# A lane's shift in four parts with in-projection blocks between them, and a unit's first state ahead of its own-chunk sums

## The chip, the cores and the metric

The kernel runs on one NeuronCore of one Trainium2 chip. The metric is the device time of one execution in microseconds (us). Engines are named as in the profile: PE is TensorE, PEld its weight load, DVE is VectorE, ACT is ScalarE, POOL is GpSimd, SP is SyncE.

## The reference

Two transformer blocks on 256 tokens of width 2048. The change touches one stage, the even mixer of the first block (an RWKV-7 scan in both directions), for context and latent tokens:

```python
def rwkv_dir_inputs(r0, k0, v0, wd, ad, mu_rkv, mu_lora, w0, w2, a0, a2, k_k, k_a, reverse):
    sh = lambda u, mu: token_shift(u.astype(jnp.float32), mu, reverse)   # u + (nb - u) * mu
    r = sh(r0, mu_rkv[0]); k = sh(k0, mu_rkv[1]); v = sh(v0, mu_rkv[2])
    w_log = -jax.nn.softplus(-(w0 + jnp.tanh(sh(wd, mu_lora[0])) @ w2)) - 0.5
    decay = jnp.exp(-jnp.exp(w_log))
    a = jax.nn.sigmoid(a0 + sh(ad, mu_lora[1]) @ a2)
    kk = hd(k * k_k)
    kk = kk * lax.rsqrt(jnp.sum(jnp.square(kk), -1, keepdims=True) + 1e-12)
    k = k * (1.0 + (a - 1.0) * k_a)
    return (hd(r), hd(decay), hd(k), hd(v), -kk, kk * hd(a))
# wkv7_scan, step by step over the tokens:
#   sa = S a;  S = S * w + sa b^T + v k^T;  y = S r
```

The inputs `r0, k0, v0, wd, ad` and a gate come from the in-projection `h @ w_in`. The rest (pooling mixer, out-projection, attention block, then a whole second block) is not touched.

## The kernel before

`order_of_work` writes one list of steps by hand. Each engine's program then walks this list and emits the instructions that it has for each step, so the list sets the order of every engine's queue. Waits between engines are semaphores, found by name.

The stage of the change is a loop over **units**. A unit is one direction `d` (a *lane*, 0 forward, 1 backward), one pair of heads `hp` and one half `seg` (context or latent), with number n = 2 hp + seg: 16 units in each lane. The generator `unit` yields 22 times: `shift`, `kk_sum`, `keys`, `turn_AV`, `P_LR`, `KR0`, `KR1`, `double0` to `double5`, `solve`, `own`, `state0` to `state3`, `centre`, `gn_sum`, `read_out`. The two lanes go in rounds, lane 1 one step behind lane 0. At the end of each round `fill` emits a number of pieces of other work, by the table

```python
FILL = {"shift": 5.5, "kk_sum": 7.5, "keys": 6, "turn_AV": 3, ..., "own": 2, "state0": 2, ...}
```

That other work is the in-projection. A **block** here is one k-tile of one sum: three PE matmuls of 128x512 (`ev_times`: high by high, high by low, low by high). Its weights come through a ring by DMA, eight blocks to a **split** (`ev_split`): ACT copies 128x1024 to the high part, DVE subtracts to get the low part. A sum of 16 blocks ends in a **copy-out**, which frees the bank: ACT's `rkv_in` or `spill_out`, or for a gate ACT's `gate_in` (tanh of the bank) and then DVE's `gate_in` (a multiply that reads the bank). All these sums share one PSUM bank (bank 0), so the first block of a sum waits until the copy-out of the sum before is done. The other filling is `mod` (`mod_row` on ACT, `mod_col` on PE and DVE).

The steps that the change touches:

* `shift(d, n, b)`. ACT: three scaled copies (k, r, v), tanh of the decay row from PSUM bank `b`, square of k (`kk_sq`, which PE's `kk_sum` waits for), scaling of the decay row (`lw`), tanh and scaling of `ag`. DVE: three multiply-adds (k, r, v), a scan (L276 helper), `be`, `er`, three tiny operations for `dc`. ACT's `kk_sum` then takes exponentials of `be`, `er`, `dc`.
* `own_chunks(d, n)`: PE makes the products of each chunk in PSUM; DVE adds to them and writes `G` and `Q`; ACT copies `HY`.
* `state(d, n, i)`, i = 0 to 3: PE multiplies the running state `S` by `G` and `Q`; DVE adds `HY` and writes the next `S`. At i = 0 DVE first sets the unit's first state: a zero (`v.zero`, helper L273) for an even n, the old state times a decay (`v.ts`, helper L264) for an odd n. PE's `state` waits for it:

```python
pe.wait_ge(*at("S", d, n, i))
pe.wait_ge(*at("G", d, n))
pe.wait_ge(*at("Q", d, n))
```

* `read_out(d, n)`: PE turns the norm's factors, DVE does three operations of 128x256.

## Time and profile before

| what | value |
|---|---|
| median of 3 runs | 3706.95 us (3701.98 to 3708.23) |
| the profiled execution, its own time | 3699.59 us |
| its span in the profile | 3697.8 us |
| mean granted clock | 0.975 of full |
| stage of the 32 units | about 147 to 1300 us |

Read the page from the top: busy shares, then the stretch of the unit stage alone, then who waits for whom there, then the timeline around single waits. Since PE's queue is in order, an idle time of PE in a timeline is a delay of everything behind it.

### The profile page before, as it was taken

How to read it: one execution, taken by the hardware profiler on the slowest of the kernel's cores; microseconds unless marked ns; L12 is line 12 of the kernel's file. 1: busy time of each engine (PE TensorE's matmuls, PEld its weight loads, DVE VectorE, ACT ScalarE, POOL GpSimd, SP SyncE). 2: the span in 40 equal slices, each digit the busy share in tenths (PEclk: the TensorE clock that was granted, in tenths of full speed). 3: DMA queues.
4: the chain of work that ended last, by engine and by line, in shares of the span. 5: the costliest groups of instructions: out<-in, count | busy, mean ns of one | idle time of the engine just before them, and what ended most of it. 6: DMA issues, size and time to landing. Idle time of an engine off the chain costs nothing. (4 is left out here: it accounts for less than half of the span.)

```text
span 3697.8 us, 71036 instructions
## 1 busy us (share of the span) xinstructions
PE 3453.2 (93%) x31368; PEld 2866.8 (78%) x31368; DVE 2045.4 (55%) x3596; ACT 1549.5 (42%) x2596; POOL 249.0 (7%) x297
## 2 busy tenths in 40 slices
PE   7998899999899989899997999899999999999998
PEld 3676677777667757777886898569898899999787
DVE  2555555565556586755656566665444555555444
ACT  2433443443334433555544443444433444444333
POOL 0011101111111130020100001010000000000000
PEclk9999999999999999999998999999999999999999
DMA  9543423443344064433334543334544455555554
GB/s 378 192 120 105 130 86 110 119 123 99 97 121 122 23 239 157 149 113 103 109 137 152 191 149 126 114 117 159 191 160 141 167 182 178 178 181 183 182 193 159
DMA packets 349472, 548.57 MB, mean 148 GB/s; under 512 B 11724, under 2 KB 119916, under 8 KB 346988
## 3 DMA queue, kind: packets, MB, share of 16 engines
q1 hardware_dynamic: 346716, 538.78, 44.1%
q8 instruction: 246, 4.03, 0.4%
q10 hardware_dynamic: 2448, 5.24, 0.4%
q14 instruction: 62, 0.51, 0.0%
HBM read 535.86 MB, written 8.13 MB: 147 GB/s over the span
## 5 line engine op out<-in xcount | busy, mean ns | idle before, releaser
L301 PE MATMUL lane<-r,r 128*128 128x256 f32 (+1 forms) x8520 | 1504.2, 326 | 36.9 <-DVE r L259 27.3
L301 PEld LDWEIGHTS lane<-r,r 128*128 128x128 f32 x8520 | 1276.4, 192 | 195.8 <-DVE r L259 35.2
L301 PE MATMUL bank<-r,r 128*128 128x512 f32 (+2 forms) x6312 | 1374.0, 357 | 53.7 <-DVE arena L267 20.0
L259 DVE TENSOR_TENSOR r<-ring,r 128x1024 fp32r<-128x1024 f32 x770 | 939.9, 1227 | 824.3 <-ACT r L298 822.9
L301 PEld LDWEIGHTS bank<-r,r 128*128 128x128 f32 (+1 forms) x6312 | 1036.4, 193 | 252.6 <-ACT arena L298 32.9
L298 ACT ACTIVATE r<-ring 128x1024 fp32r<-128x1024 f32 x770 | 808.6, 1055 | 761.9 <-PE lane L301 587.2
L301 PE MATMUL lane<-arena 64*64 64x64 f32 (+5 forms) x13068 | 577.8, 251 | 59.3 <-issue 19.4
L301 PEld LDWEIGHTS lane<-arena 64*64 64x64 f32 (+2 forms) x13068 | 431.6, 138 | 211.8 <-issue 119.9
L298 ACT ACTIVATE arena<-lane 128x256 f32<-128x256 f32 (+3 forms) x543 | 242.7, 469 | 513.8 <-PE lane L301 278.0
L259 DVE TENSOR_TENSOR arena<-arena 128x256 f32<-128x256 f32 (+6 forms) x600 | 274.3, 486 | 34.1 <-ACT arena L298 12.5
L298 ACT ACTIVATE arena<-arena 128x256 f32<-128x256 f32 (+4 forms) x366 | 153.7, 451 | 224.8 <-DVE arena L259 111.8
L270 DVE COPY arena<-lane 128x256 f32<-128x256 f32 (+2 forms) x254 | 106.6, 421 | 170.6 <-PE lane L301 141.4
L259 DVE TENSOR_TENSOR arena<-lane,arena 128x256 f32<-128x256 f32 (+2 forms) x244 | 74.9, 333 | 190.7 <-PE lane L301 189.3
L259 POOL TENSOR_TENSOR arena<-arena,cm 128x4 f32<-128x4 f32 (+1 forms) x80 | 90.9, 1136 | 1042.3 <-ACT arena L298 668.7
L304 PE MATMUL lane<-cm,arena 128*128 128x128 f32 x744 | 117.4, 284 | 27.1 <-DVE arena L259 14.3
L259 POOL TENSOR_TENSOR arena<-arena 128x256 f32<-128x256 f32 (+3 forms) x134 | 122.2, 931 | 193.7 <-DVE arena L270 99.5
L301 PE MATMUL lane<-arena,cm 64*64 64x64 f32 (+2 forms) x1440 | 125.1, 232 | 4.9 <-DVE arena L264 4.3
L304 PEld LDWEIGHTS lane<-cm,arena 128*128 128x128 f32 x744 | 88.6, 145 | 49.6 <-DVE arena L259 16.2
L259 POOL TENSOR_TENSOR st<-st,cm 128x1 f32<-128x1 f32 (+2 forms) x19 | 12.7, 671 | 1694.5 <-DVE st L264 1694.5
L298 ACT ACTIVATE r<-arena 128x256 fp32r<-128x256 f32 (+2 forms) x143 | 67.7, 478 | 102.4 <-DVE arena L267 91.5
L267 DVE SCALAR_TENSOR_TENSOR arena<-arena,vec 128x256 f32<-128x256 f32 (+1 forms) x196 | 91.7, 494 | 28.0 <-ACT arena L298 24.6
L301 PEld LDWEIGHTS lane<-arena,cm 64*64 64x64 f32 (+1 forms) x1440 | 99.3, 142 | 8.5 <-issue 6.1
(94 smaller groups left out, 1260.8 us busy)
## 6 DMA issues: line engine op xcount, KB each, us to landing
ring<-in_w_gate_up SPq DMA_DIRECT2D x88, 1024.0 KB, 4.9
ring<-in_mod_w SPq DMA_DIRECT2D x73, 1024.0 KB, 5.2
ring<-in_ev_w_in SPq DMA_DIRECT2D x44, 1024.0 KB, 8.2
ring<-in_w_down SPq DMA_DIRECT2D x44, 1024.0 KB, 5.0
ring<-in_od_w_in SPq DMA_DIRECT2D x40, 1024.0 KB, 4.9
ring<-in_w_in SPq DMA_DIRECT2D x40, 1024.0 KB, 5.0
ring<-in_w_xkv SPq DMA_DIRECT2D x32, 1024.0 KB, 5.3
ring<-in_ev_w_out SPq DMA_DIRECT2D x28, 1024.0 KB, 5.2
```

Source lines behind the costliest of these rows:

```text
L259: return Nothing() if self.e is None else self.e.tensor_tensor(o, a, b, op)
L267: return Nothing() if self.e is None else self.e.scalar_tensor_tensor(o, a, s, b, op0, op1)
L270: return Nothing() if self.e is None else self.e.tensor_copy(o, a)
L298: return self.e.activation(o, a, f, bias=bias, scale=scale)
L301: return Nothing() if self.e is None else self.e.matmul(o, l, r, start=start, stop=stop)
L304: return Nothing() if self.e is None else self.e.transpose(o, a, ident)
```

## The change

It does two things.

The step `shift` of a unit has a fourth argument `part`. Part 0 is emitted at the old place. Parts 1 to 3 go on a list `late`, and `fill` emits one of them after each piece of filling; what is left is emitted at the latest ahead of the lane's next step. On ACT the parts are: the copies for k and r; the copy for v and the tanh of the decay row; the square and `lw`; the two `ag` operations. On DVE: k and r; v; scan and `be`; `er` and the `dc` operations. The number of instructions stays.

The unit's first state is set by DVE at the start of `own_chunks`, ahead of `G` and `Q`, and no longer in `state` i = 0.

```diff
@@ -886,6 +886,8 @@
     drain(first_blocks(3, [loaded(slot_turn, 12, 4, firsts[0:2]), loaded(slot_turn, 12, 4, firsts[2:6])]))
     step("load_lora", 0)
 
+    late = []
+
     def unit(d, hp, seg):
         n = 2 * hp + seg
         t = unit_turns[d]
@@ -893,8 +895,14 @@
         if d == 0:
             lora_banks[n] = [bank(pair_turns[x][1]) for x in range(2)]
             step("lora", n, lora_banks[n])
-        step("shift", d, n, lora_banks[n][d])
+        for part in range(4):
+            if part:
+                late.append((d, n, lora_banks[n][d], part))
+            else:
+                step("shift", d, n, lora_banks[n][d], part)
         yield "shift"
+        while any(x[0] == d for x in late):
+            step("shift", *late.pop(0))
         b = bank(t)
         step("kk_sum", d, n, b)
         yield "kk_sum"
@@ -946,6 +954,8 @@
                 sources.pop(i)
             elif end:
                 due[0] = True
+            if late:
+                step("shift", *late.pop(0))
 
     def lane(d):
         for hp in range(HPS):
@@ -2226,36 +2236,38 @@
         g = M.sg[hp % 2]
         v.stt(g, g, 1.0, M.bank[b[0]], ADD, MUL).then_inc(*v.n(("free", *b), ("sg", hp)))
 
-    def shift(d, n, b):
+    def shift(d, n, b, part):
         hp, seg = divmod(n, 2)
         s = M.lane[d]
-        if n:
-            for e in ("act", "pool", "pe"):
-                v.wait_ge(*at("unit_end", d, n - 1, e))
-        own()
-        for i in (1, 0, 2):
+        bc4 = c4(s.bc)
+        ref, lst = (32, 0) if d else (31, 63)
+        if part == 0:
+            if n:
+                for e in ("act", "pool", "pe"):
+                    v.wait_ge(*at("unit_end", d, n - 1, e))
+            own()
+        for i in ((1, 0), (2,), (), ())[part]:
             src = M.rkv[hp % 2][i]
             nb = src[:, seg, 0:256] if d == 0 else src[:, seg, 2:258]
             v.wait_ge(*at("kept", d, n, i))
             v.stt((s.r, s.k, s.v)[i], nb, M.vcol("mu", (d * 3 + i) * 8 + hp), s.E3[i], MUL, ADD).then_inc(*v.n(("rkv"[i], d, n)))
-
-        st = -1 if d else 1
-        v.wait_ge(*at("lw", d, n))
-        v.scan(s.bc[:, ::st], M.C("scan"), s.lw[:, ::st]).then_inc(*v.n())
-        own()
-        bc4 = c4(s.bc)
-        ref, lst = (32, 0) if d else (31, 63)
-        v.tt(c4(s.BE[:, 0:256]), bc4, bc4[:, :, ref:ref + 1].to_broadcast([P, 4, 64]), SUB).then_inc(*v.n(("be", d, n)))
-        own()
-        v.tt(s.BE[:, 256:512], s.BE[:, 0:256], s.lw, SUB).then_inc(*v.n(("er", d, n)))
-        dl = s.dc[:, 0:4].unsqueeze(2)
-        v.tt(dl, bc4[:, :, lst:lst + 1], bc4[:, :, ref:ref + 1], SUB).then_inc(*v.n())
-        own()
-        o_, i_ = (slice(1, 4), slice(0, 3)) if d else (slice(0, 3), slice(1, 4))
-        v.tt(dl[:, o_], dl[:, o_], bc4[:, i_, ref:ref + 1], ADD).then_inc(*v.n())
-        own()
-        first = 3 if d else 0
-        v.cp(s.dc[:, 4:5], bc4[:, first, ref:ref + 1]).then_inc(*v.n(("dc_in", d, n)))
+        if part == 2:
+            st = -1 if d else 1
+            v.wait_ge(*at("lw", d, n))
+            v.scan(s.bc[:, ::st], M.C("scan"), s.lw[:, ::st]).then_inc(*v.n())
+            own()
+            v.tt(c4(s.BE[:, 0:256]), bc4, bc4[:, :, ref:ref + 1].to_broadcast([P, 4, 64]), SUB).then_inc(*v.n(("be", d, n)))
+        if part == 3:
+            v.wait_ge(*at("be", d, n))
+            v.tt(s.BE[:, 256:512], s.BE[:, 0:256], s.lw, SUB).then_inc(*v.n(("er", d, n)))
+            dl = s.dc[:, 0:4].unsqueeze(2)
+            v.tt(dl, bc4[:, :, lst:lst + 1], bc4[:, :, ref:ref + 1], SUB).then_inc(*v.n())
+            own()
+            o_, i_ = (slice(1, 4), slice(0, 3)) if d else (slice(0, 3), slice(1, 4))
+            v.tt(dl[:, o_], dl[:, o_], bc4[:, i_, ref:ref + 1], ADD).then_inc(*v.n())
+            own()
+            first = 3 if d else 0
+            v.cp(s.dc[:, 4:5], bc4[:, first, ref:ref + 1]).then_inc(*v.n(("dc_in", d, n)))
 
     def kk_sum(d, n, b):
         s, hp = M.lane[d], n // 2
@@ -2324,6 +2336,12 @@
 
     def own_chunks(d, n, bp):
         s = M.lane[d]
+        if n % 2 == 0:
+            v.zero(s.S[0]).then_inc(*v.n(("S", d, n, 0)))
+        else:
+            v.wait_ge(*at("dc", d, n))
+            v.wait_ge(*at("S", d, n - 1, 4))
+            v.ts(s.S[1], s.S[0], s.dc[:, 4:5], None, MUL).then_inc(*v.n(("S", d, n, 0)))
         full(bp[0])
         v.wait_ge(*at("DI", d, n))
         cq = lambda ap: ap.rearrange("p (c q n) -> p q c n", c=2, q=2)
@@ -2334,13 +2352,6 @@
     def state(d, n, i, by):
         s, seg = M.lane[d], n % 2
         x = 3 - i if d else i
-        if i == 0:
-            if seg == 0:
-                v.zero(s.S[0]).then_inc(*v.n(("S", d, n, 0)))
-            else:
-                v.wait_ge(*at("dc", d, n))
-                v.wait_ge(*at("S", d, n - 1, 4))
-                v.ts(s.S[1], s.S[0], s.dc[:, 4:5], None, MUL).then_inc(*v.n(("S", d, n, 0)))
         if not (seg == 1 and i == 3):
             v.wait_ge(*at("y_mm", d, n, i))
             v.wait_ge(*at("HY", d, n))
@@ -3126,26 +3137,29 @@
             a.wait_ge(*at("mix_out", hp - 2))
         a.act(M.sg[hp % 2], M.bank[b[0]], ACT.Tanh, scale=0.5).then_inc(*a.n(("gate_tanh", hp)))
 
-    def shift(d, n, b):
+    def shift(d, n, b, part):
         s, hp, w = M.lane[d], n // 2, d * 8 + n // 2
-        if n:
-            for e in ("dve", "pool", "pe"):
-                a.wait_ge(*at("unit_end", d, n - 1, e))
-        a.wait_ge(*at("derived"))
-        for i in (1, 0, 2):
+        if part == 0:
+            if n:
+                for e in ("dve", "pool", "pe"):
+                    a.wait_ge(*at("unit_end", d, n - 1, e))
+            a.wait_ge(*at("derived"))
+        for i in ((1, 0), (2,), (), ())[part]:
             m = (d * 3 + i) * 8 + hp
             a.wait_ge(*at("rkv", hp, i))
             a.act(s.E3[i], M.rkv[hp % 2][i][:, n % 2, 1:257], ACT.Copy, scale=M.omu[:, m:m + 1]).then_inc(*a.n(("kept", d, n, i)))
-        full(b)
-        a.act(s.lw, M.bank[b[0]][:, 0:256], ACT.Tanh, scale=0.5, bias=M.w0h[:, w:w + 1]).then_inc(*a.n())
-        tanh = a.last()
-        a.wait_ge(*at("k", d, n))
-        a.act(s.sq, s.k, ACT.Square, scale=M.vcol("k_k", hp)).then_inc(*a.n(("kk_sq", d, n)))
-        a.wait_ge(*tanh)
-        a.act(s.lw, s.lw, ACT.Copy, scale=C1, bias=C1).then_inc(*a.n(("lw", d, n)))
-        a.act(s.ag, M.bank[b[0]][:, 256:512], ACT.Tanh, scale=0.5, bias=M.a0h[:, w:w + 1]).then_inc(*a.n(("free", *b)))
-        own()
-        a.act(s.ag, s.ag, ACT.Copy, scale=0.5, bias=0.5).then_inc(*a.n(("ag", d, n)))
+        if part == 1:
+            full(b)
+            a.act(s.lw, M.bank[b[0]][:, 0:256], ACT.Tanh, scale=0.5, bias=M.w0h[:, w:w + 1]).then_inc(*a.n(("lw_tanh", d, n)))
+        if part == 2:
+            a.wait_ge(*at("k", d, n))
+            a.act(s.sq, s.k, ACT.Square, scale=M.vcol("k_k", hp)).then_inc(*a.n(("kk_sq", d, n)))
+            a.wait_ge(*at("lw_tanh", d, n))
+            a.act(s.lw, s.lw, ACT.Copy, scale=C1, bias=C1).then_inc(*a.n(("lw", d, n)))
+        if part == 3:
+            a.act(s.ag, M.bank[b[0]][:, 256:512], ACT.Tanh, scale=0.5, bias=M.a0h[:, w:w + 1]).then_inc(*a.n(("free", *b)))
+            own()
+            a.act(s.ag, s.ag, ACT.Copy, scale=0.5, bias=0.5).then_inc(*a.n(("ag", d, n)))
 
     def head_root(d, n, b, name):
 
```

PE's, POOL's and SP's orders are the same as before. On ACT and DVE the order differs at three kinds of place.

DVE around the own chunks of unit 2 (the third of 16), both lanes. `arena<-lane,arena 128x2x2x64 x2` is `G` and `Q`, `MEMSET` the first state, `arena<-lane,arena 128x64` a next state, `r<-ring,r 128x1024` the low part of a split. Before:

```order
L259 TENSOR_TENSOR arena<-lane,arena 128x2x2x64 x2
L267 SCALAR_TENSOR_TENSOR arena<-arena,vec 128x256
L259 TENSOR_TENSOR r_1024_60<-ring,r_1024_59 128x1024
L273 MEMSET arena 128x64
L259 TENSOR_TENSOR arena<-lane,arena 128x64
L259 TENSOR_TENSOR arena<-lane,arena 128x2x2x64 x2
L259 TENSOR_TENSOR arena<-lane,arena 128x64
L273 MEMSET arena 128x64
```

and now, the same stretch:

```order
L273 MEMSET arena 128x64
L259 TENSOR_TENSOR arena<-lane,arena 128x2x2x64 x2
L267 SCALAR_TENSOR_TENSOR arena<-arena,vec 128x256
L259 TENSOR_TENSOR r_1024_60<-ring,r_1024_59 128x1024
L259 TENSOR_TENSOR arena<-lane,arena 128x64
L273 MEMSET arena 128x64
L259 TENSOR_TENSOR arena<-lane,arena 128x2x2x64 x2
```

The first state of lane 0 moved ahead of lane 0's `G` and `Q` and so of the split; that of lane 1 moved ahead of lane 1's `G` and `Q` and of the next state of lane 0 (the `128x64` behind them).

ACT around lane 0's shift of unit 14: `omu` marks the three scaled copies, `lane,small` the tanh of the decay row and of `ag`, `bank 128x512` the copy-out `gate_in`, `r<-ring` the high part of a split. Before:

```order
L298 ACTIVATE arena<-arena,omu 128x256 x3
L298 ACTIVATE arena<-lane,small 128x256
L298 ACTIVATE arena<-arena,vec 128x256
L298 ACTIVATE arena<-arena 128x256
L298 ACTIVATE arena<-lane,small 128x256
L298 ACTIVATE arena<-arena 128x256
L298 ACTIVATE arena<-bank 128x512
L298 ACTIVATE r_1024_61<-ring 128x1024
```

and now:

```order
L298 ACTIVATE arena<-arena,omu 128x256 x2
L298 ACTIVATE arena<-bank 128x512
L298 ACTIVATE arena<-arena,omu 128x256
L298 ACTIVATE arena<-lane,small 128x256
L298 ACTIVATE arena<-arena,vec 128x256
L298 ACTIVATE arena<-arena 128x256
L298 ACTIVATE arena<-lane,small 128x256
L298 ACTIVATE arena<-arena 128x256
L298 ACTIVATE r_1024_61<-ring 128x1024
```

The copy-out moved from behind the eight instructions of the shift to behind the second.

DVE at the same place; `arena,vec 128x256` are multiply-adds, `cm,arena` the scan, `lane 128x256` begins lane 1's `read_out`, `arena,bank 128x512` is `gate_in`. Before:

```order
L267 SCALAR_TENSOR_TENSOR arena<-arena,vec 128x256 x4
L276 SCALAR_TENSOR_TENSOR arena<-cm,arena 128x256
L259 TENSOR_TENSOR arena<-arena 128x256 x2
L259 TENSOR_TENSOR arena<-arena 128x4
L259 TENSOR_TENSOR arena<-arena 128x3
L270 COPY arena<-arena 128x1
L270 COPY arena<-lane 128x256
L259 TENSOR_TENSOR arena<-arena 128x256
L267 SCALAR_TENSOR_TENSOR arena<-arena,vec 128x256
L267 SCALAR_TENSOR_TENSOR arena<-arena,bank 128x512
L259 TENSOR_TENSOR r_1024_62<-ring,r_1024_61 128x1024
```

and now:

```order
L267 SCALAR_TENSOR_TENSOR arena<-arena,vec 128x256 x3
L270 COPY arena<-lane 128x256
L259 TENSOR_TENSOR arena<-arena 128x256
L267 SCALAR_TENSOR_TENSOR arena<-arena,vec 128x256
L267 SCALAR_TENSOR_TENSOR arena<-arena,bank 128x512
L267 SCALAR_TENSOR_TENSOR arena<-arena,vec 128x256
L276 SCALAR_TENSOR_TENSOR arena<-cm,arena 128x256
L259 TENSOR_TENSOR arena<-arena 128x256 x2
L259 TENSOR_TENSOR arena<-arena 128x4
L259 TENSOR_TENSOR arena<-arena 128x3
L270 COPY arena<-arena 128x1
L259 TENSOR_TENSOR r_1024_62<-ring,r_1024_61 128x1024
```

Lane 1's `read_out` and the copy-out now come ahead of v, the scan and what follows it.

Over the stage the orders show 12 places where a split moved from behind a shift to between its parts, 7 where a copy-out did, 2 where a `mod_row` did, and 15 where DVE's `read_out` of lane 1 now stands ahead of parts 1 to 3 of lane 0's shift.

## Rows read from the trace of the kernel before

**Rows 1.** The page, part 1: busy time of each engine.

```profile
PE 3453.2 (93%) x31368; PEld 2866.8 (78%) x31368; DVE 2045.4 (55%) x3596; ACT 1549.5 (42%) x2596; POOL 249.0 (7%) x297
```

**Rows 2.** Stretch by stretch: length, busy and instruction count by engine, PEclk, DMA share, GB/s.

```profile
147.00:1300.00 1153.00, 1076.19 (x17065) 819.50 (x17064) 648.08 (x1618) 465.45 (x1033) 144.34 (x158) 0.98 0.35 105
```

**Rows 3.** Waits of PE from 147 to 1300 us: total us, times, longest us.

```profile
PE lane L301 <- issue: 19.9, 20, 2.8
PE bank L301 <- DVE arena L267: 16.0, 6, 4.4
PE bank L301 <- ACT arena L298: 14.7, 8, 4.7
PE lane L301 <- DVE arena L264: 10.8, 10, 2.0
PE lane L301 <- DVE arena L273: 8.0, 10, 1.9
```

**Rows 4.** Timeline, DVE then PE, 340 to 347 us: start, length, what [idle before].

```profile
340.79 1.23 DVE L259 TENSOR_TENSOR r<-ring,r 128x1024 fp32r<-128x1024 f32 x1 [1.71 <-ACT r L298]
341.98 0.11 DVE L273 MEMSET arena<- 128x64 f32 x1
...
346.19 0.11 DVE L273 MEMSET arena<- 128x64 f32 x1
...
342.15 1.85 PE L301 MATMUL lane<-arena 64*64 64x64 f32 x104 [1.79 <-DVE arena L273]
...
346.36 0.45 PE L301 MATMUL lane<-arena 64*64 64x64 f32 x8 [0.40 <-DVE arena L273]
```

**Rows 5.** Timeline, DVE then PE, 848 to 855 us.

```profile
851.94 1.22 DVE L259 TENSOR_TENSOR r<-ring,r 128x1024 fp32r<-128x1024 f32 x1 [1.61 <-ACT r L298]
...
853.52 0.45 PE L301 MATMUL lane<-arena 64*64 64x64 f32 x8 [2.02 <-DVE arena L264]
```

**Rows 6.** Timeline, PE, then ACT, then DVE, 1171 to 1182 us.

```profile
1177.42 3.67 PE L301 MATMUL bank<-r,r 128*128 128x512 f32 x9 [3.23 <-DVE arena L267]
...
1174.08 0.58 ACT L298 ACTIVATE arena<-bank 128x512 f32<-128x512 f32 x1
...
1174.12 1.16 DVE L259 TENSOR_TENSOR arena<-arena 128x256 f32<-128x256 f32 x4
...
1175.38 0.41 DVE L270 COPY arena<-lane 128x256 f32<-128x256 f32 x1
...
1176.69 0.68 DVE L267 SCALAR_TENSOR_TENSOR arena<-arena,bank 128x512 f32<-128x512 f32 x1
```

**Rows 7.** Timeline, ACT, then PE, 951 to 960 us.

```profile
953.12 0.45 ACT L298 ACTIVATE arena<-lane,small 128x256 f32<-128x256 f32 x1
...
955.47 0.58 ACT L298 ACTIVATE arena<-bank 128x512 f32<-128x512 f32 x1
...
956.10 4.15 PE L301 MATMUL bank<-r,r 128*128 128x512 f32 x10 [3.45 <-ACT arena L298]
```

**Rows 8.** Short stretches, columns as in rows 2.

```profile
956.25:959.66 3.41, 3.41 (x9) 2.64 (x10) 1.76 (x5) 0.74 (x1) 0.00 (x0) 0.50 1.14 333
1000.62:1004.03 3.41, 3.41 (x89) 3.10 (x78) 0.88 (x3) 0.36 (x1) 0.00 (x0) 0.50 0.02 5
1148.20:1151.60 3.40, 3.40 (x112) 2.80 (x112) 0.98 (x3) 0.60 (x1) 0.00 (x0) 1.00 0.02 5
```

**Rows 9.** Timeline, PE, ACT, then DVE, 284 to 298 us.

```profile
285.05 3.70 PE L301 MATMUL bank<-r,r 128*128 128x512 f32 x15
288.59 0.50 PE L301 MATMUL lane<-cm,arena 128*128 128x2 f32 x4
...
289.29 1.02 ACT L298 ACTIVATE arena<-arena 128x256 f32<-128x256 f32 x3
291.60 0.41 ACT L298 ACTIVATE arena<-arena 128x256 f32<-128x256 f32 x1 [1.28 <-POOL arena L259]
...
286.19 0.69 DVE L276 TENSOR_TENSOR_SCAN arena<-cm,arena 128x256 f32<-128x256 f32 x1 [2.00 <-ACT arena L298]
```

## The prediction

> **What bounds the kernel now.** I read four views, from coarse to fine. The page says that PE is busy for 93% of the span and no other engine for more than 55% [rows 1], so time can only be gained where PE stands idle or runs slowly. The stretch view gives the stage of the 32 units: 1153 us long, PE busy for 1076, so some 77 us of idle time, at a mean granted clock of 0.98 [rows 2]. DMA moves 105 GB/s at a busy share of 0.35 there, which leaves it out of the question. The waits of PE in that stage say what ended the idle time [rows 3]: 19.9 us are "issue" (nothing that the profile shows; PE's own instruction stream does not change, so I leave them as they are), 16.0 and 14.7 us stand ahead of blocks in PSUM bank 0, and 10.8 and 8.0 us are ended by helpers L264 and L273, which are the two ways of setting a unit's first state. PE's queue is in order: an idle time there delays all that follows, and a wait removed there shortens the kernel unless another wait opens behind it. The change aims at both kinds of wait, 49.5 us in all.
>
> **Term 1: the first state.** The timeline shows two patterns. In the first the zero or scaling sits on DVE behind the low part of a split. At 341.98 the MEMSET takes 0.11 us but starts only when the 1.23 us split is done, which itself waited 1.71 us for ACT; PE stood idle for 1.79 us for it [rows 4]. In lane 1 of unit 9 the same costs 2.02 us [rows 5]. There are seven of these, 1.4 to 2.0 us each. In the second pattern, 13 times, lane 1's first state stands behind lane 0's next state, which waits for PE; PE pays 0.40 us, as at 346.36, or 0.49 with the scaling [rows 4]. The order shows that the instruction now stands ahead of `G` and `Q`. These are done well before the split starts, so after the change PE waits for nothing there. What is late next is the next state of lane 0, which stays behind the split. In the pattern of rows 4 it comes some 0.3 us after the split's end at 342.02. PE, starting 1.79 us earlier, is then still in lane 1's own chunks and two blocks, and needs that state at about 343.7. In the pattern of rows 5 it is nearer: the state is ready at about 853.3, and PE wants it, two blocks after a start at 851.5, at about 853.5. So I count all of it: 10.8 + 8.0 = **18.8 us**, and 14 as the lower end, if the three waits of the tight pattern come back in good part. The upper end is 18.8 too. The added waits of the scaling (for the decays and for the unit before's last state) are for things long finished at that point, and I price them at nothing; if they were not, `G` and `Q` would queue behind them.
>
> **Term 2: the copy-outs.** Of the 30.7 us ahead of blocks only those count whose copy-out moved relative to the shift.
> Lane 0, unit 14: PE stood idle 3.23 us from 1174.19, until DVE's multiply of 1176.69 [rows 6]. The multiply stood behind the scan, the 1.16 us of four operations and the tiny copy behind them, and the `read_out` from 1175.38 on, 1.31 us long. Now it stands behind k, r and `read_out` alone, and both its input and the sum come from PE work that was done before PE fell idle at 1174.19. ACT's tanh (0.58 us, at 1174.08) can come a microsecond earlier, since the piece of `mod` that PE runs between the sum's end and the idle time takes that long. So the multiply can start at about 1174.1: gain 2.6 us.
> Lane 1, unit 11: ACT's copy started at 955.47 behind the shift; the tanh of the decay row ended at 953.57, and the copy now comes right there, since the sum had ended before PE fell idle at 952.65 [rows 7]: 1.9 us of the 3.45. Lane 1 of unit 2 is the same pattern: 1.9 us more.
> Lane 0, unit 10: the multiply moves ahead of `er` and the `dc` operations, 1.16 + 0.15 less one operation of 0.42 (the rows of these instructions in unit 14 [rows 6]): 0.9 us.
> Lane 0, unit 5: the copy now follows its sum at once, and a wait of half a microsecond goes. The other two moved copies started as soon as their sum was done, or had no wait of PE behind them: nothing. One copy-out comes about 0.1 us later, because a split went into its shift without pulling it forward.
> Sum 2.6 + 3.8 + 0.9 + 0.5 = **7.8 us**, with 3 and 10 as ends. The 4.44 us wait of unit 4 and four further ones of 1.3 to 3.2 us have a copy-out whose place against the shift is the same. They stay.
>
> **Term 3: the clock.** Behind long waits PE's granted clock falls from 2.4 to 1.2 GHz. In the stretch from 956.25, right after the wait of 3.45 us, PEclk is 0.50 and nine matmuls run in 3.41 us [rows 8], where 15 take 3.70 us at the full clock, 0.247 us each [rows 9]. That is 3.41 - 9 x 0.247 = 1.2 us lost. The stretch from 1000.62 lies behind a first-state wait of 1.89 us and is at 0.50 too; the one from 1148.20, behind a wait of 1.90 us, is at 1.00 [rows 8]. Such a fall is thus likely but not sure after waits of 1.9 us and more. Six lie behind waits that terms 1 and 2 remove or cut by a good part (at 294, 854, 881, 956, 1001 and 1178 us). I take five of them: 5 x 1.2 = **6.0 us**, with ends of 0 and 10.
> The Trainium skill says otherwise on this term (TensorE: Matmul & The Clock Gate, Part 1: The HAM clock gate): the ramp's penalty is under 1% of a typical span, and one should not fit to a specific count. By that the term is left out and the kernel comes to 3682 us; the rows above show the loss for this kernel, so the sum keeps it.
>
> **Term 4: what the parts delay.** Twelve splits now stand inside a shift: up to 1.05 us on ACT and 1.22 on DVE ahead of the rest of it. And in lane 0 DVE's `read_out` of lane 1 (1.31 us) goes ahead of v and the scan. Behind these wait the exponentials of ACT, then `keys` on DVE, then PE's `turn_AV` and `P_LR`. The cover can be read in unit 2 of lane 0. DVE stood idle 2.00 us before the scan at 286.19, which is where `read_out` now runs. ACT took the exponentials at 289.29, over a microsecond after DVE had their input, because it first waited for PE's sums at 288.59. And it then stood idle another 1.28 us until 291.60 for POOL's power [rows 9]. A delay of the scan by a `read_out` and a split, 2.5 us less the idle time used, ends inside this cover. PE's own entry to the lane, the sums at 288.59, needs only the square, which ACT issues before `lw` and behind no more than one split. The cover is thinner in lane 1, where a split costs about a microsecond of a like slack. I take **-1.5 us**; ends are 0 and 12 splits of 1.22 us, -15.
>
> **Sum.** 18.8 + 7.8 + 6.0 - 1.5 = 31.1 us. Against the profiled execution's own 3699.6 us that is 3668.5. That execution lies 7.4 us under the median of the runs, so the median should go from 3706.95 to about **3676 us**. All later stages are unchanged and start earlier. A difference of under 0.2% (7.4 us) can hardly be told from none.
>
> **Rivals.**
> *Only the first state counts.* A copy pulled ahead on ACT waits there for its sum and holds back the shift behind it, so that the lane loses what the bank gains. For it: in units 5 and 14 of lane 0 the copy stands behind only two instructions of the shift. Against it: the sums end within a microsecond or so of that point. Then 18.8 plus two falls of the clock, 2.4, remain: 3686 us.
> *The lanes get late.* PE waits at `turn_AV` or `P_LR` in about half of the twelve units with a moved split, and 10 to 20 us are given back: 3687 to 3697 us. Against it speak the 1.28 and 2.00 us of rows 9.
> *Given back.* PE reaches each later wait sooner, and these are bound by something that did not move, such as POOL's power or the weights' DMA. Then the idle time moves to other rows and the total stays: 3704 us. Against it: all these chains begin with PE's own sums, and the DMA share is 0.35 [rows 2].
> *Slower.* `read_out` ahead of the scan, 15 times 1.31 us, and twelve splits of 1.22 us reach PE in full: 34.3 us lost against 26.6 gained by terms 1 and 2, and no clock comes back: 3706.95 + 7.7, about 3715 us. This decides once the cover, the 2.00 us before the scan and the 1.28 us before the last ACT step, is smaller than the 2.5 us put in; in rows 9 it is 3.3.
>
> **How the numbers follow.** Forecast (gain 20 to 42 us): 0.66. Only the first state: 0.12. Lanes late: 0.10. Given back: 0.08. Slower: 0.04. The range runs from the sum of upper ends, 18.8 + 10 + 10 = 39 us and 5 for the scatter of the medians, 3663 us, to the lower ends 14 + 3 with 5 given back by the lanes, 3695 us; this takes in the first rival and most of the second. Faster by over 0.2%: 0.66 + 0.12 + 0.10 = 0.88; within 0.2%: 0.08; slower: 0.04.
>
> **What would show it.** In the waits of PE over the stage, the rows ended by L264 and L273 should be gone or under 2 us together; those on bank 0 should fall from 30.7 to about 23 us, with the idle time near 1177 under 1 us; PEclk should fall less often. The scan in lane 0 should start about 1 us later against PE's blocks, with `read_out` ahead of it. Waits of PE's lane steps ended by DVE's L259 or L267 of more than 5 us in all would speak for the second rival; unchanged total idle time with other names, for the third. The forecast is wrong if PE's idle time of some 77 us in the stage falls by less than 15.

## The result, and the profile after

The changed kernel takes **3658.46 us** (median of 4 runs, 3650.43 to 3661.35), against 3706.46 us for the kernel before on the same chip (3701.98 to 3708.23). The ratio is 0.9875, with a 95% interval of 0.986 to 0.9889. That is 48.0 us less, where the prediction said 31 and allowed at most 44. The direction was right, and the time is 4.5 us below the low end of the range. The profiled execution took 3658.94 us, against 3699.59 before: 40.7 us less.

The page, part 1, answers to [rows 1]:

```profile
PE 3438.2 (94%) x31368; PEld 2859.2 (78%) x31368; DVE 2047.9 (56%) x3596; ACT 1550.6 (42%) x2596; POOL 243.9 (7%) x297
```

All instruction counts are the same, and PE is busy for 15.0 us less (3453.2 to 3438.2). Less idle time cannot do that. Something makes the same instructions shorter.

A fixed window like that of [rows 2] holds more work after the change. So I cut both kernels at the same two instructions instead: the first product of unit 0's `lora`, and the last long wait of the stage, the one of 3.86 us ahead of the last `read_out`. Between them lies the same work. The stretch view of the kernel before for that stretch (columns as in rows 2):

```profile
144.05:1302.39 1158.34, 1079.15 (x17082) 821.78 (x17081) 650.77 (x1624) 469.33 (x1043) 145.34 (x159) 0.98 0.35 105
```

And of the changed kernel:

```profile
147.42:1259.78 1112.36, 1063.58 (x17081) 811.90 (x17081) 652.90 (x1624) 470.08 (x1043) 140.06 (x159) 0.99 0.37 110
```

The stage is **46.0 us** shorter (1158.34 to 1112.36). PE's idle time gives 30.4 of it (79.2 to 48.8), and 15.6 us are busy time (1079.15 to 1063.58) for the same matmuls. These two numbers are read for every run below. "The stage" is this stretch from here on.

The waits of PE in the changed kernel, 147 to 1270 us, beside [rows 3]:

```profile
PE lane L301 <- issue: 18.8, 24, 2.8
PE bank L301 <- DVE arena L267: 11.4, 6, 4.1
PE bank L301 <- ACT arena L298: 9.8, 8, 3.1
...
PE lane L301 <- DVE arena L259: 3.5, 14, 0.3
PE lane L301 <- ACT arena L298: 0.2, 1, 0.2
```

The rows of L264 and L273, 18.8 us, are gone. Bank 0 fell from 30.7 to 21.2 us. The lane steps wait for L259 14 times, 0.3 us at most, so the lanes were not made late.

The place of [rows 4], in the timeline of the changed kernel, 334 to 341 us:

```profile
335.30 1.78 PE L301 MATMUL lane<-arena 64*64 64x64 f32 x97
335.82 1.22 DVE L259 TENSOR_TENSOR r<-ring,r 128x1024 fp32r<-128x1024 f32 x1 [1.71 <-ACT r L298]
...
337.14 0.11 DVE L273 MEMSET arena<- 128x64 f32 x1
337.74 0.34 PE L301 MATMUL lane<-arena 64*64 64x64 f32 x7 [0.66 <-issue]
```

DVE's split at 335.82 still waits 1.71 us for ACT, exactly as before. PE no longer does: the 104 matmuls that stood behind the 1.79 us of [rows 4] (lane 0's first state step and lane 1's own chunks) now start at 335.30, ahead of the split, without a wait for DVE. The MEMSET at 337.14 is that of lane 1, ahead of the products that need it.

The place of [rows 6], unit 14 of lane 0, 1135 to 1139 us, PE, then ACT, then DVE:

```profile
1137.59 2.33 PE L301 MATMUL bank<-r,r 128*128 128x512 f32 x9 [0.41 <-DVE arena L267]
...
1136.22 0.60 ACT L298 ACTIVATE arena<-bank 128x512 f32<-128x512 f32 x1 [2.33 <-PE bank L301]
...
1136.85 0.69 DVE L267 SCALAR_TENSOR_TENSOR arena<-arena,bank 128x512 f32<-128x512 f32 x1
...
1138.31 0.69 DVE L276 TENSOR_TENSOR_SCAN arena<-cm,arena 128x256 f32<-128x256 f32 x1 [0.38 <-ACT arena L298]
```

The multiply from the bank now stands ahead of the scan, 0.63 us behind ACT's tanh (2.61 before), and PE's wait fell from 3.23 to 0.41 us. The place of [rows 7], unit 11 of lane 1:

```profile
928.00 0.58 ACT L298 ACTIVATE arena<-bank 128x512 f32<-128x512 f32 x1
...
928.64 1.66 PE L301 MATMUL bank<-r,r 128*128 128x512 f32 x6 [1.66 <-ACT arena L298]
```

Here the wait fell from 3.45 to 1.66 us, as the copy stands ahead of the last four of ACT's instructions of the shift.

The stretches where PEclk (the granted clock as a share of the full one) is 0.50 add up, inside the stage, to 52.6 us in 14 falls before, and to 28.1 us in 7 falls after. Of that PE was busy for 48.3 us before and for 23.9 after. The rest of the slow time lies in the wait itself. In the changed kernel the clock was already down while PE stood idle: its wait of 4.11 us ended at 445.27, and the fall began at 443.25. In this stretch PE is busy for 2.35 of 4.37 us.

```profile
443.25:447.62 4.37, 2.35 (x6) 1.86 (x7) 3.07 (x6) 0.00 (x0) 0.00 (x0) 0.50 1.00 352
```

### The profile page after: what moved, and what is told of

It is laid out like the page before. It is cut to its first block and busy times, and to the rows that moved or that the text cites. A ratio compares the mean times of both kernels' runs of the same rounds, so it can differ in the third digit from the quotient of the medians.

```text
span 3657.1 us, 71068 instructions
## 1 busy us (share of the span) xinstructions
PE 3438.2 (94%) x31368; PEld 2859.2 (78%) x31368; DVE 2047.9 (56%) x3596; ACT 1550.6 (42%) x2596; POOL 243.9 (7%) x297
## 5 line engine op out<-in xcount | busy, mean ns | idle before, releaser
L259 DVE TENSOR_TENSOR r<-ring,r 128x1024 fp32r<-128x1024 f32 x770 | 940.1, 1227 | 827.3 <-ACT r L298 825.9
L301 PEld LDWEIGHTS bank<-r,r 128*128 128x128 f32 (+1 forms) x6312 | 1028.2, 191 | 239.9 <-ACT arena L298 28.7
L259 DVE TENSOR_TENSOR arena<-arena 128x256 f32<-128x256 f32 (+7 forms) x600 | 273.6, 485 | 36.2 <-ACT arena L298 14.0
L259 DVE TENSOR_TENSOR arena<-lane,arena 128x256 f32<-128x256 f32 (+2 forms) x244 | 74.7, 334 | 167.3 <-PE lane L301 165.7
L259 POOL TENSOR_TENSOR arena<-arena,cm 128x4 f32<-128x4 f32 (+1 forms) x80 | 84.1, 1051 | 1006.3 <-ACT arena L298 633.0
L259 POOL TENSOR_TENSOR arena<-arena 128x256 f32<-128x256 f32 (+3 forms) x134 | 123.8, 944 | 195.5 <-DVE arena L270 100.5
L304 PEld LDWEIGHTS lane<-cm,arena 128*128 128x128 f32 x744 | 89.9, 146 | 50.2 <-DVE arena L259 16.3
L259 POOL TENSOR_TENSOR st<-st,cm 128x1 f32<-128x1 f32 (+2 forms) x19 | 12.7, 671 | 1695.2 <-DVE st L264 1688.0
L267 DVE SCALAR_TENSOR_TENSOR arena<-arena,vec 128x256 f32<-128x256 f32 (+1 forms) x196 | 93.6, 500 | 23.3 <-ACT arena L298 18.1
```

The costliest lines, as they stand in the source:

```text
L259: return Nothing() if self.e is None else self.e.tensor_tensor(o, a, b, op)
L267: return Nothing() if self.e is None else self.e.scalar_tensor_tensor(o, a, s, b, op0, op1)
L301: return Nothing() if self.e is None else self.e.matmul(o, l, r, start=start, stop=stop)
L304: return Nothing() if self.e is None else self.e.transpose(o, a, ident)
```

## The experiments

The two theories at the outset were these. **A**: the two edits are independent; each takes away its own waits, and the clock gives back more than the 6 us that I took. **B**: they need each other. Later runs asked what the parts of a shift must look like on each engine, what a longer wait costs in full, and whether the 21 us still left at bank 0 can be had.

All runs in one table. The stage and its busy time come from the stretch view between the same two instructions; idle time is their difference; "at half" is the time with a granted clock of 0.50 in the stage while PE was busy, added up from the trace. The experiments ran in three sets, each on a chip of its own beside the kernel before, whose medians there were 3699.95 us (each edit alone, ScalarE only, no blocks between), 3701.25 us (changed again, VectorE only, copy-outs three times, hold after eight blocks) and 3703.07 us (before again, the other two holds); "against before" is the ratio within a set, with its 95% interval.

| run | median us | against before | stage us | busy | idle | at half |
|---|---|---|---|---|---|---|
| before (first profile) | 3706.46 | | 1158.3 | 1079.2 | 79.2 | 48.3 |
| before again | 3701.82 | 0.9997 [0.9985, 1.0008] | 1157.2 | 1075.7 | 81.5 | 42.9 |
| changed | 3658.46 | 0.9875 [0.986, 0.9889] | 1112.4 | 1063.6 | 48.8 | 23.9 |
| changed again | 3655.68 | 0.9877 [0.9864, 0.989] | 1113.0 | 1064.1 | 48.9 | 24.0 |
| first state alone | 3676.09 | 0.9933 [0.9919, 0.9948] | 1127.6 | 1068.8 | 58.8 | 33.8 |
| parts alone | 3688.31 | 0.9967 [0.9954, 0.998] | 1142.2 | 1069.8 | 72.4 | 32.3 |
| parts on ScalarE only | 3670.78 | 0.9918 [0.9904, 0.9933] | 1127.8 | 1066.4 | 61.4 | 26.4 |
| parts on VectorE only | 3679.47 | 0.9938 [0.9926, 0.9949] | 1133.3 | 1072.5 | 60.8 | 42.6 |
| parts, no blocks between | 3673.57 | 0.9929 [0.9911, 0.9946] | 1129.0 | 1069.0 | 59.9 | 32.6 |
| copy-outs three times | 3690.39 | 0.9965 [0.9952, 0.9978] | 1138.9 | 1069.6 | 69.3 | 33.9 |
| hold after eight blocks | 3663.89 | 0.9901 [0.9888, 0.9914] | 1114.5 | 1064.3 | 50.2 | 27.0 |
| hold after a sum | 3663.72 | 0.9896 [0.9877, 0.9916] | 1113.1 | 1063.5 | 49.6 | 25.3 |
| hold after a gate | 3661.47 | 0.9891 [0.9873, 0.991] | 1113.9 | 1063.8 | 50.1 | 22.0 |

### Each edit alone

First state alone: the changed kernel with `shift` in one piece again, on every engine and in `unit` and `fill`.

```diff
-        for part in range(4):
-            if part:
-                late.append((d, n, lora_banks[n][d], part))
-            else:
-                step("shift", d, n, lora_banks[n][d], part)
+        step("shift", d, n, lora_banks[n][d])
```

> The kernel before with the first state alone moved ahead of own_chunks. Theory A (the two halves of the change act on separate waits of TensorE, and the gain is the idle time removed plus the clock that comes back behind it): TensorE's idle time ended by the first state goes from 18.7 to under 1 us, waits of its weight load that the sum left out give 3 to 4 us more, and about two falls of the clock go, so 23 to 28 us less than before, about 3681 us. The waits on bank 0 stay at 30 to 31 us. Theory B (the extra gain over the forecast comes from the two halves together, through the clock): this half alone gives only its 18.8 us or less, about 3688 us. Theory C (most of the gain belongs to the first state): over 35 us.

Parts alone: the changed kernel with the first state set in `state`, at i == 0, again.

```diff
     def own_chunks(d, n, bp):
-        if n % 2 == 0:
-            v.zero(s.S[0]).then_inc(*v.n(("S", d, n, 0)))
-        else:
...
+        if i == 0:
+            if seg == 0:
+                v.zero(s.S[0]).then_inc(*v.n(("S", d, n, 0)))
```

> The change with the first state put back into the state step, so the shift in parts alone. Theory A: the waits on bank 0 fall from 31 to about 21.5 us as in the change, the first state's waits stay at 18 to 19, and the clock gives 6 to 12 us back: 16 to 22 us less than before, about 3687 us, and the gains of this run and of the first state alone add up to that of the change (48 us) within 5 us. Theory B: this alone gives 10 us or less, and the two add up to under 35.

The changed kernel was timed again, five rounds on another chip.

> The changed kernel as it stands, timed on the chip of this set of runs. Theory A (the two edits add, and half of the time at the half clock is lost): the kernel before minus 46 to 48 us, so about 3652 to 3662, as in its first run. Theory B (the part beyond the two edits alone, -24 and -12 us, was the difference between two chips): the kernel before minus 36 to 40 us.

The waits of PE with the first state alone, 147 to 1300 us:

```profile
PE bank L301 <- DVE arena L267: 16.0, 6, 4.4
PE bank L301 <- ACT arena L298: 14.7, 8, 4.7
```

With the parts alone:

```profile
PE bank L301 <- DVE arena L267: 11.4, 6, 4.1
PE lane L301 <- DVE arena L264: 10.8, 10, 2.1
PE bank L301 <- ACT arena L298: 9.8, 8, 3.1
PE lane L301 <- DVE arena L273: 8.3, 10, 1.9
```

Each edit takes exactly its own rows. The first state alone leaves bank 0 at 30.7 us, the value before; the parts alone leave the first state at 19.1 us and bring bank 0 to 21.2, the value of both together. In the stage the gains are 30.7 and 16.1 us. Their sum, 46.8, is the 46.0 (second profile: 45.3) of both. Theory A holds in the stage.

Theory B has the whole times on its side: the medians give 23.9 and 11.6 us (theory A had 16 to 22 for the parts), 35.5 together, where both edits give 45.6 on the chip of the second set. Two things can account for most of that, though no run separates them. First, outside the stage the two profiles of the kernel before have 2539.5 and 2538.8 us (span less stage), while all eleven profiles with an edit have 2542.4 to 2546.4. So some 3 to 8 us are given back elsewhere, once per kernel, whichever edit it has; a sum of two single edits counts it twice. Second, the four to thirteen runs of a kernel scatter by 2 to 20 us. Part of the 3 to 8 us lies ahead of the stage, where nothing was changed: 144.1 and 143.2 us in the kernel before, 143.5 to 147.4 with an edit. Behind it there are 2395.4 and 2395.7 us before and 2397.3 to 2402.5 with an edit. One piece of that can be named, with the traces laid side by side matmul by matmul. At 1929 us the kernel before waits 2.47 us for a split and runs on at the full clock, in both profiles. The changed kernel has the same wait at 1887 us, 2.48 us long, and a fall of the clock behind it, which costs 1.5 us. Ten of the eleven profiles with an edit have that fall, at 1.5 to 1.6 us each. So part of what is given back is the clock again, at a wait that no edit touches; what takes the rest was not tried.

### The kernel before, profiled again

> The kernel before as it stands, for a second profile of it. Theory A (the first profile stands for the kernel; its two parts add): unit stage 1162 to 1166 us with 55 to 60 us at the half clock. Theory B (before was profiled on its slow side, and the parts are worth more together, by some 10 us, than -24 and -12 us alone): unit stage 1157 to 1161 us, half-clock time 48 to 53 us.

By the bounds written there the result lies with theory A in length, and just below its edge, between the two theories, in half-clock time. (Those bounds are for a stage counted to the last `read_out` product, 6.2 us later than in the table: 1163.4 us, with 54.6 us at the half clock.) The idle time by kind of wait is the same in both profiles, to 0.1 us for bank 0 (16.0 and 14.8 us) and to 0.3 us for the first state (10.8 and 8.3 us). The falls are not: 14 in one, 10 in the other.

### Parts on one engine only

ScalarE's shift in four parts, VectorE's whole at part 0:

```diff
     def shift(d, n, b, part):
+        if part == 0:
+            for q in range(4):
+                shift_part(d, n, b, q)
+
+    def shift_part(d, n, b, part):
```

> The change, but VectorE does its whole shift at part 0, so only ScalarE's order is in parts. If ScalarE's queue alone held the copy-outs back, the copy-outs by rkv_in and spill_out (units 2, 5 and 11) keep their gain of some 6 us and only the gates (units 10 and 14) lose theirs, since the multiply on VectorE stands behind the shift again and that shift now waits for ScalarE's late parts: their waits return to 2 to 3.5 us or more. 4 to 8 us slower than the change, 3663 to 3667 us. If the order of VectorE (read_out ahead of the scan) gave part of the gain by itself, it is slower by over 10 us.

The same edit in ScalarE's `shift` instead:

> The changed kernel, but ScalarE does its whole shift at part 0; only VectorE's shift stands in parts. Theory A (on ScalarE the copy-outs rkv_in and spill_out stand behind the shift again, on VectorE gate_in does not): waits of ScalarE on bank 0 go back up by 5 to 7 us, those of VectorE stay near 11, total 8 to 11 us above the changed kernel. Theory B (with the other half run, in which ScalarE alone had parts, the whole gain of the parts was lost, so each engine's parts are worth something only with the other's): bank 0 waits 29 to 31 us in all and the time some 12 us above the changed kernel. Theory C (VectorE's order carries it all, ScalarE's parts are idle): within 3 us of the changed kernel.

| bank 0 waits of PE, us | ended by ACT | ended by DVE |
|---|---|---|
| before | 14.7 | 16.0 |
| parts on both | 9.8 | 11.4 |
| parts on ScalarE only | 10.9 | 19.2 |
| parts on VectorE only | 15.6 | 17.0 |

Both missed: I expected 3663 to 3667 us for the first, and it took 3670.78. By its number (12.3 us above 3658.46) that run falls to the other theory of its text, that VectorE's order brings part of the gain by itself; the second run speaks against this, since VectorE's parts alone bring nothing. For the second, theory B of its text came nearest on the waits, with 32.6 us of them where it said 29 to 31; the cost of 23.8 us against the changed kernel was twice what any theory said, since 18.6 us more ran at the half clock. Parts on one engine leave bank 0 at 30.1 and 32.6 us, no better than the 30.7 without any, and one place for each shows why. Parts on ScalarE only, unit 14 of lane 0, ACT, DVE, then PE:

```profile
1141.64 0.60 ACT L298 ACTIVATE arena<-bank 128x512 f32<-128x512 f32 x1 [2.33 <-PE bank L301]
...
1143.72 0.69 DVE L276 TENSOR_TENSOR_SCAN arena<-cm,arena 128x256 f32<-128x256 f32 x1 [0.58 <-ACT arena L298]
...
1147.02 0.68 DVE L267 SCALAR_TENSOR_TENSOR arena<-arena,bank 128x512 f32<-128x512 f32 x1
...
1147.76 2.50 PE L301 MATMUL bank<-r,r 128*128 128x512 f32 x5 [5.16 <-DVE arena L267]
```

ACT's tanh is early (1141.64), but it pushed ACT's decay row back, and DVE's whole shift, in front of the multiply, waits for that row. The multiply comes 5.38 us behind the tanh, and PE waits 5.16 us, more than the 3.23 of [rows 6]. Parts on VectorE only, unit 12 of lane 1:

```profile
1019.09 1.04 ACT L298 ACTIVATE r<-ring 128x1024 fp32r<-128x1024 f32 x1
1020.04 0.58 ACT L298 ACTIVATE arena<-bank 128x512 f32<-128x512 f32 x1
1020.16 1.23 DVE L259 TENSOR_TENSOR r<-ring,r 128x1024 fp32r<-128x1024 f32 x1 [1.91 <-ACT r L298]
...
1021.70 0.68 DVE L276 TENSOR_TENSOR_SCAN arena<-cm,arena 128x256 f32<-128x256 f32 x1
...
1023.68 0.68 DVE L267 SCALAR_TENSOR_TENSOR arena<-arena,bank 128x512 f32<-128x512 f32 x1
1024.42 0.80 PE L301 MATMUL bank<-r,r 128*128 128x512 f32 x1 [4.91 <-DVE arena L267]
```

Now ACT's split of the weights (1019.09) stands behind ACT's whole shift, DVE's half of the split waits 1.91 us for it, and scan and multiply queue behind. PE waits 4.91 us, 2.92 with parts on both. In both places the two queues have copy-out, split and shift in different orders, and the wait of one engine for the other reaches PE.

### No blocks between the parts

```diff
     def fill(n):
+        while late:
+            step("shift", *late.pop(0))
```

> The change, but all late parts are emitted at the start of the fill, with no block between them. What stays of the change is the first state and VectorE's read_out of lane 1 ahead of parts 1 to 3 of lane 0. Theory A: as the first state alone, 3681 us, with the waits on bank 0 near 30 us; read_out's place gives 0 to 2 us through the gates of units 10 and 14. If the gain of the parts is read_out's place and not the blocks between, this run keeps nearly the whole gain, about 3660 us.

The parts follow one another, only `read_out` of the other lane still stands between. Bank 0 is back at 28.7 us (14.5 ended by ACT, 14.2 by DVE) and the time, 3673.57 us, is within 3 us of that of the first state alone. So the gain of the parts comes from the copy-outs that stand between them; `read_out`'s new place brings 2.0 us of wait at most.

### What a longer wait costs in full

The changed kernel, with `rkv_in` and `gate_in` of ScalarE done three times each:

```diff
+        for _ in range(2):
+            a.act(M.rkv[hp % 2][i][:, :, 1:257], seg2(M.bank[b[0]]), ACT.Copy).then_inc(*a.n())
+            own()
         a.act(M.rkv[hp % 2][i][:, :, 1:257], seg2(M.bank[b[0]]), ACT.Copy).then_inc(*a.n(("free", *b), ("rkv", hp, i)))
```

> The changed kernel with each ScalarE copy-out of rkv_in and gate_in done three times over, two more of 0.59 us each plus the gap between them, about 1.25 us, at 28 sums in the stage. From the time that each bank had been free before the next product, TensorE's idle time grows by about 25 us. Theory A (a wait also costs what the clock falls for: half of the time at the half clock): half-clock time in the unit stage rises from 34 to 50 to 65 us and the total by 25 plus 8 to 15, so 33 to 40 us. Theory B (the clock falls are not tied to these waits): half-clock time stays within 5 us of 34, total plus 24 to 28. Theory C (the lanes wait for each other anyway and take the waits up): total less than plus 18.

Its waits of PE, 147 to 1300 us:

```profile
PE bank L301 <- ACT arena L298: 24.3, 19, 4.4
PE lane L301 <- issue: 20.6, 27, 3.2
PE bank L301 <- DVE arena L267: 15.2, 7, 4.1
```

The waits on bank 0 rose from 21.2 to 39.5 us. Against the changed kernel's profile from the same chip, idle time in the stage rose by 20.4 us (25 expected) and busy time by 5.5 for the same matmuls, about half of the 9.9 us more that were busy at the half clock. So a wait costs more than its idle time, as theory A says. But A expected 16 to 31 us more at the half clock, and B at most 5; the 9 to 10 us lie between. A's mechanism shows, its size does not. The medians differ by 34.7 us, the stages of the two profiles by 26.0. Of the other 9 us, 2.5 lie outside the stage, and 6.3 come from which runs were profiled: this kernel's lies 4.7 us under its median, the changed kernel's 1.6 us above. Runs of this kernel go from 3677.7 to 3692.5. Theory C, in which the lanes take the waits up, is out.

### Can the rest be had?

In `fill`, once a sum has ended and the due piece of the modulation is issued, the rest of the share is kept for the next round, so that two lane steps cover the copy-out:

```diff
+            was = due[0]
             i = len(sources) - 1 if due[0] else 0
             due[0] = False
...
+            if was and len(sources) > 1:
+                break
```

> The changed kernel, but in fill, once a sum has ended and the due piece of the modulation is issued, the rest of the share is held back to the next round, so that two lane steps stand between the copy-out and the next block. Theory A: TensorE's waits on bank 0 fall from 21 to 3 to 8 us, half-clock time from 34 to about 25, total 15 to 22 us below the changed kernel. Rival (given back: the blocks held back leave the lane steps without cover, so lanes wait for VectorE and ScalarE instead): waits on lane banks rise by 8 us or more, total within 6 us of the changed kernel.

In this form it holds after every eight blocks. The second form holds only after a whole sum, the third only behind `gate_in`; both mark the end in `products`, and `fill` holds on that mark alone:

```diff
-                yield j == len(u.blocks) - 1
+                yield 2 if end else j == len(u.blocks) - 1
```

> The changed kernel, but after a whole sum and its piece of the modulation the rest of the share waits for the next round (the earlier such kernel did this after every eight blocks, so twice as often, and its lanes then waited 14 us at kk_sum). Theory A (only the needless holds did the harm): bank 0 waits 21 to about 4 us, kk_sum waits under 6 us, total 6 to 14 us below the changed kernel. Rival (each hold that falls near kk_sum gives its gain back): kk_sum and keys waits over 9 us, total within 4 us of the changed kernel or above it.

> The changed kernel with the hold only behind gate_in, whose bank needs ScalarE and VectorE in turn (VectorE's waits on bank 0: 11.4 us). Theory A: those 11 us fall to 1 to 3, kk_sum waits stay under 3 us, total 6 to 12 us below the changed kernel, 2 to 4 us of it from the clock. Rival: the sums behind shift against the lanes, ScalarE's waits on bank 0 grow from 9.8 to over 16 us, total within 4 us.

The waits of PE with the hold after eight blocks:

```profile
PE lane L301 <- issue: 20.2, 26, 2.6
PE lane L301 <- ACT arena L298: 14.4, 12, 2.6
...
PE bank L301 <- DVE arena L267: 1.9, 2, 1.6
...
PE bank L301 <- ACT arena L298: 0.7, 1, 0.7
```

With the hold after a sum:

```profile
PE lane L301 <- ACT arena L298: 9.8, 7, 2.6
...
PE bank L301 <- DVE arena L267: 5.2, 3, 2.3
...
PE lane L301 <- DVE arena L267: 2.6, 1, 2.6
PE bank L301 <- ACT arena L298: 2.2, 3, 1.0
```

Bank 0 falls as theory A says, from 21.2 to 2.6 us, and in the second form to 7.4, where it had about 4. But a row that was 0.2 us in the changed kernel is now 14.4 and 9.8: the lane's sums wait for ACT's square. In the changed kernel the blocks issued behind the copy-out (seven of them, 21 matmuls, in one stretch at 572.73) ran while ACT came to the square. Held back, they no longer cover it, as in unit 6 of lane 1 with the hold after a sum:

```profile
573.61 1.28 DVE L267 SCALAR_TENSOR_TENSOR arena<-arena,vec 128x256 f32<-128x256 f32 x3
574.13 0.51 ACT L298 ACTIVATE arena<-arena,vec 128x256 f32<-128x256 f32 x1 [0.48 <-DVE arena L267]
...
574.69 1.01 PE L301 MATMUL lane<-cm,arena 128*128 128x2 f32 x4 [2.60 <-ACT arena L298]
```

All three end with the stage at 1113 to 1115 us, where it was, and with times 3 to 8 us above 3655.68 or 3658.46. For the first two the rival of their texts holds: the idle time moves from the bank to the lane (the first is even 8.2 us slower, where the rival had it within 6). The third fits neither of its theories. Its bank 0 rows ended by VectorE fell from 11.4 to 6.5 us only, those ended by ScalarE stayed at 9.8, where the rival had over 16, and the lane's wait for ACT rose from 0.2 to 3.6 us, with 2.6 us more for DVE's L267. The total, 3661.47 us, is no gain either. No version tried here beats the changed kernel.

## Why the prediction fell short

**Term 1, first state, 18.8 us: right in idle time, short by the weight loads.** PE's two rows went from 18.8 to nothing, and the "14" of the low end was not needed. But the wait has a part that PE's rows do not hold. PEld's rows of the kernel before, 147 to 1300 us, read

```profile
PEld lane L301 <- DVE arena L264: 12.7, 10, 2.3
PEld lane L301 <- DVE arena L273: 10.3, 11, 2.2
```

that is 23.0 us, 4.2 more than [rows 3] gives for PE. With the first state set ahead, the matmuls of the `state` steps take 37.3 us without their idle time, where they took 40.9: 3.7 us. It is 3.7 too with the first state alone, and nothing with the parts alone. That the edit brings these 3.7 us is shown; that they are the weight loads is argued from the 4.2.

**Term 2, copy-outs, 7.8 us: 9.5 measured.** By place: unit 14 of lane 0 gave 2.8 (2.6 taken), unit 11 of lane 1 1.8 (1.9), unit 10 1.1 (0.9), unit 5 0.5 (0.5). Unit 2 of lane 1 gave 3.0, from 4.67 to 1.64 us, where I had taken 1.9 by likeness to unit 11. The others changed by 0.35 us or less either way. The rival "only the first state counts" is out: with the first state alone bank 0 keeps its 30.7 us.

**Term 3, the clock, 6.0 us: this is the term that failed most, 12.2 measured.** It was right that falls go with the waits, and wrong in number and price. I took five falls of 1.2 us each. In the stage there were 14 before (10 in the second profile) and 7 after (6). The busy time at half clock fell by 24.4 us, from 48.3 to 23.9, and half of that is lost time: 12.2 us, or 9.5 from the second profile. Per fall that left, it is 1.7 us or more. The 1.2 came from nine matmuls counted in a single stretch of 3.41 us [rows 8]. The timeline that I had beside it says more, since it does not cut matmuls at an edge: ten in 4.15 us [rows 7], less 10 x 0.247, is 1.7 us. And some falls last twice as long. By the first profiles even the upper end of the term, 10, was too low; by the second it just held. That half of it is lost can be tested over all 13 profiles of the table. A least-squares fit of busy time on "at half", with one more constant for the three profiles that still have the old first state, gives 0.51 us per us (standard error 0.04) and 2.2 us for the first state (0.7), and no profile is off by more than 1.2 us. The 2.2 is less than the 3.7 counted above; the fit leaves up to 1.5 us open between clock and first state. The Trainium skill says that the ramp's penalty is under 1% of a typical span and that one should not fit to a specific count (TensorE: Matmul & The Clock Gate, Part 1: The HAM clock gate). For a single ramp this agrees: in the kernel before, the first fall, at 31 us, has PE busy for 6.0 us at the half clock, about 3 us lost, 0.1% of the span. For all falls together it does not: over the whole span there are 33, with 181.5 us at the half clock, of which PE is busy for 131.7; half of that, an estimate by the 0.51 of the stage, is 66 us, 1.8%. And what the change got back of it in the stage, 12.2 us, is a quarter of what it brought there, so for the worth of a change it must stand in the sum. That one should not fit to a count is borne out by the kernel before, with PE busy at the half clock for 48.3 and 42.9 us, in 14 and 10 falls, for the same waits.

**Term 4, delay by the parts, -1.5 us: not seen.** The stretch of [rows 9] in the changed kernel, PE, ACT, then DVE:

```profile
285.22 3.70 PE L301 MATMUL bank<-r,r 128*128 128x512 f32 x15
288.75 0.50 PE L301 MATMUL lane<-cm,arena 128*128 128x2 f32 x4
...
289.53 1.74 ACT L298 ACTIVATE arena<-arena 128x256 f32<-128x256 f32 x4
...
285.50 0.42 DVE L270 COPY arena<-lane 128x256 f32<-128x256 f32 x1 [1.54 <-PE lane L304]
...
287.21 1.22 DVE L259 TENSOR_TENSOR r<-ring,r 128x1024 fp32r<-128x1024 f32 x1
288.35 0.68 DVE L276 TENSOR_TENSOR_SCAN arena<-cm,arena 128x256 f32<-128x256 f32 x1
```

`read_out` (285.50) and a split (287.21) stand ahead of the scan, as the order said. Measured from the 15 blocks, the scan starts at +3.13 us, where it was +1.14: 2.0 us later, where I had written about 1. ACT takes the exponentials at +4.31, against +4.24. The cover took all of it, and the lane rows of L259 add to 3.5 us in waits of 0.3. So "the lanes get late" and "slower" are out.

**Sum.** In the stage: 18.6 us of first state, 9.5 of bank 0 and 2.3 of other idle time, together 30.4; then 12.2 us of clock and 3.4 left in the busy time, which is the weight loads' 3.7 but for 0.3. That is the 46.0. Outside the stage 5.2 us came back (2539.5 to 2544.7), which no term had. Of these, 3.4 us lie ahead of the stage, where nothing was changed, and 1.9 behind it; only the latter can be a sign of the rival "given back", and they are a small part of its size. 46.0 - 5.2 = 40.8, the 40.7 of the two profiled executions. The forecast for these was 31.1, so the terms miss by 9.6 us: 6.2 too little for the clock, 3.7 for the weight loads and 2.3 of other idle time put at nothing, 1.7 too little for the copy-outs, 1.5 for the delay that did not come, less the 5.2 and half a microsecond of small terms. The other part of the miss, as large as the clock's, is how it was carried over to the medians: I added the 7.4 us by which the profiled execution of the kernel before lay below its median, while the changed kernel's lies within 0.5 us of its own. That is chance of which run is profiled, and no mechanism. Without it the forecast would have been 3668.5 us, still 10 above what was measured. For this chip's medians the gain was 48.0 us, for those of the second set 45.6.

## What to carry to other kernels

Price a wait of TensorE at more than its idle time: add half of the busy time that the trace shows at the half clock behind such waits, over the whole stage and not from one stretch, and look at the weight loads' rows beside the matmuls', which are longer. When a chain on one engine is cut into parts so that urgent work can go between, cut it in the same places on every engine that shares the chain; with one half alone the bank waits were back at 30 us and more. And before moving cover to one wait, name what it covers now: the blocks held back after eight blocks or a sum emptied the bank's rows and filled the lane's, and PE's idle time in the stage ended 0.8 to 1.4 us above the 48.8 of the changed kernel.

## What the runs showed of the hardware

The same wait does not always bring a fall of the clock. Two profiles of the kernel before agree in each kind of wait to 0.1 us for bank 0 and 0.3 us for the first state, and have 52.6 and 48.8 us at the half clock in 14 and 10 falls.

Waits ended by "issue", for which no engine can be named, are part of it. In the changed kernel three of them, of 2.50, 2.52 and 2.81 us, stand in `double` at 320, 600 and 955 us, and the granted clock falls to 0.50 at each. All 13 profiles have them at the same places, within eleven matmuls (lane 1 of units 2 and 11, lane 0 of unit 6), 2.2 to 4.0 us each, whatever the edit. The second profile of the changed kernel has two of the three without a fall. Two more, of about 2 us in units 3 and 12 of lane 0, stand in both profiles of the kernel before and with the parts alone, and not in the changed kernel nor with the first state alone (the one in unit 3 came back in the first two kernels with a hold); no term of mine had them. What causes these waits was not tried, but the DMA records of the traces point to PE's instructions themselves. The page lists a queue of kind "instruction", q8, with 246 packets of 16 KB for PE's 31368 matmuls and as many weight loads. In the 13 profiles 46 waits of this kind in the stage are longer than 1.9 us. In every one, a packet of q8 starts between 0.7 us ahead of the wait's start and 1.5 us behind it, and PE goes on 1.2 to 1.6 us after that packet has landed (of the matmuls of the stage at large, 7 in 100 stand in that span behind a packet by chance). The places fit too: in the changed kernel the three long waits lie 34 and 42 times 127 matmuls apart, and shorter ones near them one or a few times 127. And these packets came late: in the 2 us ahead of each, other transfers kept the DMA engines busy at a share of 0.73 to 1.18, while most instruction packets of the stage met idle ones (median 0.0). So these waits, 2 to 4 us each with a fall of the clock behind some, look like TensorE waiting for its own instructions behind weight transfers. No run moved such a transfer, so this is read from the traces and not shown by an experiment.
